# A hybrid attention, convolution and expert layer: chunk-by-chunk waits ahead of two matmul stages, and a shared last step

## The reference, cut to what matters

```python
h = rms_norm(x, norm1) * (1.0 + sc1) + sh1
q, k, v, u = project(h, w_in, q_norm, k_norm)
attn = context_attention(...) or latent_attention(...)   # 512 wide
conv = conformer_conv(u, ...)                            # 512 wide
x = x + g1 * (jnp.concatenate([attn, conv], axis=-1) @ w_out)
h2 = rms_norm(x, norm2) * (1.0 + sc2) + sh2
x = x + g2 * peer(h2, peer_wq, peer_keys, peer_u, peer_v)

def conformer_conv(u, w_dw, b_dw, ln_g, ln_b, w_pw):
    ...                                    # gated, then a depthwise convolution: y
    y = jax.nn.silu(layer_norm(y, ln_g, ln_b))
    return y @ w_pw
```

## Time and profile before

| what | us |
|---|---|
| median of 3 runs (lowest to highest) | 1766.24 (1764.96 to 1771.95) |
| the profiled execution's own time | 1766.6 |
| its span, first to last instruction | 1764.8 |
| PE busy in it | 1672.8 |
| DVE busy in it | 1558.7 |
| ACT busy in it | 861.6 |
| POOL busy in it | 644.9 |

### The profile page before, as it was taken

One profiled execution on the slowest core, in us unless ns is written; L12 is line 12 of the kernel. 1 busy time (PEld: TensorE's weight loads), 2 busy tenths in 40 slices (PEclk: granted clock), 3 DMA queues, 4 the chain that ended last, 5 costly groups with the idle time before them and its releaser, 6 DMA issues.

```text
span 1764.8 us, 29813 instructions
## 1 busy us (share of the span) xinstructions
PE 1672.8 (95%) x9344; PEld 1408.6 (80%) x9344; DVE 1558.7 (88%) x3209; ACT 861.6 (49%) x2416; POOL 644.9 (37%) x636
## 2 busy tenths in 40 slices
PE   6999998999957887999999999999999999999997
PEld 4566776966636776999999999999998998999986
DVE  3887863389999987999999999999999999999999
ACT  3221563337787876444444444444444444444443
POOL 0000000033548884444344444344444443443441
PEclk9999999999987998999999999999999999999999
DMA  8343102211114789999999999999999999999996
GB/s 352 119 146 118 73 1 75 72 49 60 48 42 161 195 265 314 405 408 400 399 409 398 395 413 400 399 410 399 402 411 393 393 402 400 397 404 408 398 385 213
DMA packets 128788, 508.79 MB, mean 288 GB/s; under 512 B 8528, under 2 KB 63568, under 8 KB 79312
## 3 DMA queue, kind: packets, MB, share of 16 engines
q0 software_dynamic: 36864, 268.45, 37.5%
q1 hardware_dynamic: 91568, 239.37, 36.5%
q10 hardware_dynamic: 288, 0.13, 0.0%
HBM read 480.00 MB, written 27.92 MB: 288 GB/s over the span
## 4 chain that ended last, share of the span: by engine, by line
DVE 33%; DMA 23%; PE 22%; issue 18%; POOL 2%; ACT 1%; DVEq 1%; POOLq 0%; SPq 0%; ACTq 0%
DMA slab<-table,ixr 21%; DVE slab L1604 9%; PE psum L461 7%; DVE ulo L1517 5%; PE psum L693 3%; DVE slab L1554 3%; DVE slab L1593 3%; PE psum L781 2%; DVE vlo L1580 2%; DVE slab L1588 2%; PE psum L462 2%; DVE wlo L1576 2%; PE psum L624 1%; POOL slab L1697 1%; DVE slab L1431 1%
## 5 line engine op out<-in xcount | busy, mean ns | idle before, releaser
L1697 POOL DMA_INDIRECT slab<-table,ixr x256 | 422.9, 1652 | 619.7 <-DVE slab L1604 547.3
L802 PE MATMUL psum<-hhi,uhi 128*128 128x384 f32 x1008 | 339.0, 336 | 1.1 <-issue 0.9
L802 PE MATMUL psum<-hhi,ulo 128*128 128x384 f32 x1008 | 338.2, 336 | 0.0
L802 PE MATMUL psum<-hlo,uhi 128*128 128x384 f32 x1008 | 337.6, 335 | 0.0
L1593 DVE SCALAR_TENSOR_TENSOR slab<-slab,h2tok 128x1024 f32<-128x1024 f32 x256 | 312.7, 1222 | 27.6 <-DMA slab<-table,ixr 27.6
L1604 DVE SCALAR_TENSOR_TENSOR slab<-slab,cf 128x1024 f32<-128x1024 f32 x252 | 323.7, 1284 | 14.5
L816 PE MATMUL psum<-vhi,whi 128*128 128x512 f32 x768 | 299.8, 390 | 11.2 <-DVE wlo L1576 11.2
L816 PE MATMUL psum<-vhi,wlo 128*128 128x512 f32 x768 | 302.3, 394 | 0.0
L816 PE MATMUL psum<-vlo,whi 128*128 128x512 f32 x768 | 302.0, 393 | 0.0
L461 PE MATMUL psum<-slab 128*128 128x512 f32 x464 | 240.6, 600 | 6.9 <-ACT slab L943 5.2
L1104 ACT CAST whi<-slab 128x384 fp32r<-128x384 f32 x128 | 65.8, 514 | 307.2 <-DVE slab L1588 307.2
(11 more groups left out here) (216 smaller groups left out, 2790.4 us busy)
## 6 DMA issues: line engine op xcount, KB each, us to landing
slab<-ublk SPq DMA_DIRECT2D x64, 1024.0 KB, 8.6
slab<-vtab SPq DMA_DIRECT2D x64, 1024.0 KB, 8.4
slab<-wblk SPq DMA_DIRECT2D x90, 512.0 KB, 4.5
slab<-g_dram SPq DMA_DIRECT2D x32, 768.0 KB, 9.2
g_dram<-slab SPq DMA_DIRECT2D x11, 2048.0 KB, 9.1
slab<-table,ixr POOLq DMA_INDIRECT x256, 9.2
x<-x_in SPq DMA_DIRECT2D x1, 2560.0 KB, 10.7
y_out<-x SPq DMA_DIRECT2D x5, 512.0 KB, 3.5
```

The source lines that it names most:

```text
L802: last = pe.matmul(psum[:, b, 0:ND], w[:, c, :], m[:, c, :], start=(m_ == 0), stop=(m_ == 3 * DC - 1))
L1697: pool.indirect_dma_start(out=rows[:, sl % GR, :], out_offset=None, in_=table, in_offset=bass.IndirectOffsetOnAxis(ap=ixr[:, half, sl % 8: ...
```

## The change

Three edits. (1) ScalarE's gate of chunk 0 stands ahead of the last two attention copies, the other three behind them, and the first pw block waits for each chunk of `y` at its use. (2) The first output block waits for seven chunks of `mlo` at its head and for the eighth at its use. (3) At the end, of each dense tile VectorE takes the low four chunks alone; the high four are scaled by ScalarE from PSUM to SBUF (`scaled_out`) and added to `x` by GpSimd. The transposes use more PSUM banks, in an order written out by hand; ScalarE's copies of the dense sums wait for `row_used` in place of `summed`; the last tile is stored in two halves.

```diff
@@ tensor
-            def linear(dst, w, src, chunks=DC, p0=T_L, fresh=None):
+            def linear(dst, w, src, chunks=DC, p0=T_L, fresh=None, gated=False):
                 for c in range(chunks):
                     if fresh is not None:
                         pe.wait_ge(h_ready, fresh + c + 1)
+                    if gated:
+                        pe.wait_ge(y_ready, c + 1)
                     last = both(dst, w[:, c, :], src[:, c, :], 0, p0, c == 0, c == chunks - 1)
...
-            pe.wait_ge(y_ready, CC)
             pe.wait_ge(tp_read, 4 * N_UNITS)
             for b in range(2):
                 pe.wait_ge(attn_ready, N_UNITS - 1 + b)
-                linear(lin[b % 2], weights(S_PW + b), y, CC, YP)
+                linear(lin[b % 2], weights(S_PW + b), y, CC, YP, gated=not b)
...
-            pe.wait_ge(mix_lo, DC)
-
             def out_block(j):
                 pe.wait_ge(out_lo, j + 1)
                 pe.wait_ge(lin_dve, max(j - 1, 0) + 1)
+                if not j:
+                    pe.wait_ge(mix_lo, DC - 1)
                 for c in range(DC):
+                    if not j and c == DC - 1:
+                        pe.wait_ge(mix_lo, DC)
...
-            for k in range(TILES):
-                if k < N_GATHER:
-                    pe.wait_ge(summed, k + 1)
-                else:
-                    pe.wait_ge(evacuated, k - N_GATHER + 1)
-                for half in range(2):
-                    if k:
-                        pe.wait_ge(fin_read, DC * (k - 1) + 4 * half + 4)
-                    for c in range(4):
-                        last = pe.transpose(psum[:, half, ...], final_src(k)[...], ident)
-                    last.then_inc(fin_tp, 1)
+            pe.wait_ge(summed, 1)
+            turn(0, 0)
+            turn(0, 1)
+            pe.wait_ge(evacuated, 1)
+            turn(2, 1)
+            pe.wait_ge(summed, 2)
+            turn(1, 0)
+            pe.wait_ge(evacuated, 2)
+            turn(1, 1)
+            pe.wait_ge(fin_read, 4)
+            turn(2, 0)
+            turn(3, 1)
+            pe.wait_ge(fin_read, 8)
+            turn(3, 0)
+            pe.wait_ge(evacuated, 3)
+            pe.wait_ge(fin_scaled, 4)
+            turn(4, 1)
+            pe.wait_ge(fin_read, 12)
+            turn(4, 0)
@@ scalar
                 lay(un)
-                if un:
+                if 0 < un < N_UNITS - 1:
                     mixed(un - 1)
-            mixed(N_UNITS - 1)
-            for c in range(CC):
+
+            def gate(c):
                 act.wait_ge(yscaled, c + 1)
                 act.activation(y[:, c, :], y[:, c, :], ACT.Silu, bias=V(V_LB + c), scale=V(V_LG + c)).then_inc(y_ready, 1)
+
+            gate(0)
+            mixed(N_UNITS - 2)
+            mixed(N_UNITS - 1)
+            for c in range(1, CC):
+                gate(c)
...
+            act.wait_ge(out_done, KEYS)
+            act.wait_ge(row_used, N_GATHER * SLOTS)
+            evacuate(2)
+            evacuate(3)
+            scale_out(0, 3)
+            evacuate(4)
+            scale_out(1, 7)
+            scale_out(2, 9)
@@ vector
-            for k in range(TILES):
-                ...
+            take(0, 0, 1)
+            take(0, 1, 2)
+            take(1, 0, 4)
+            take(1, 1, 5)
+            take(2, 0, 6)
+            take(3, 0, 8)
+            take(4, 0, 10)
@@ gpsimd
+            for n in range(N_DENSE):
+                for j in range(4):
+                    pool.wait_ge(fin_scaled, 4 * n + j + 1)
+                    xc, _ = final_x(N_GATHER + n, 4 + j)
+                    pool.tensor_tensor(xc, xc, scaled_out[:, 4 * n + j, :], ALU.add).then_inc(fin_added, 1)
@@ sync
+            for k in range(N_GATHER):
+                sp.wait_ge(fin_read, DC * (k + 1))
+                store(k, slice(0, DC))
+            for n in range(N_DENSE - 1):
+                sp.wait_ge(fin_read, DC * N_GATHER + 4 * (n + 1))
+                sp.wait_ge(fin_added, 4 * (n + 1))
+                store(N_GATHER + n, slice(0, DC))
+            sp.wait_ge(fin_added, 4 * N_DENSE)
+            store(TILES - 1, slice(4, DC))
+            sp.wait_ge(fin_read, DC * N_GATHER + 4 * N_DENSE)
+            store(TILES - 1, slice(0, 4))
+            sp.wait_ge(stored, 16 * (TILES + 1))
```

More of the change, by code:

```diff
@@ L268, in build @@
         wgt = view(36864, 4, ND)
+        scaled_out = view(33792, 4 * N_DENSE, P)
         slab_at = nc.lookup_mloc(slab).addr
@@ L301, in build @@
         ix_copied = sem("ix_copied"); dots = sem("dots"); gelued = sem("gelued"); coef = sem("coef");
-        summed = sem("summed"); evacuated = sem("evacuated"); fin_tp = sem("fin_tp"); fin_read = sem("fin_read"); stored = sem("stored")
+        summed = sem("summed"); evacuated = sem("evacuated"); fin_tp = sem("fin_tp"); fin_read = sem("fin_read"); fin_scaled = sem("fin_scaled"); fin_added = sem("fin_added"); stored = sem("stored")
         kv_stored = sem("kv_stored")
@@ L328, in hot_a_split, with final_bank, final_x @@
             return 1 if b % 4 == 3 else 2
+        def final_bank(k, half):
+            own = [2 + 2 * ORDER[N_GATHER + n] for n in range(N_DENSE)]
+            return {(0, 0): 0, (0, 1): 1, (2, 1): own[0], (1, 0): own[0] + 1, (1, 1): own[1], (2, 0): 0,
+                    (3, 1): own[1] + 1, (3, 0): 1, (4, 1): own[0], (4, 0): own[0] + 1}[k, half]
+        def final_x(k, c):
+            t = ORDER[k]
+            return x[:, c, t * P:(t + 1) * P], mod[:, M_G2 + c, int(t == TP):int(t == TP) + 1]
         def final_src(k):
@@ L424, in _, with store @@
             load_quad(quads - 1, 1, True)
-            for k in range(TILES):
+            def store(k, cols):
                 t = ORDER[k]
+                sp.dma_start(y_out[:, cols, t * P:(t + 1) * P], x[:, cols, t * P:(t + 1) * P]).then_inc(stored, 16)
+            for k in range(N_GATHER):
                 sp.wait_ge(fin_read, DC * (k + 1))
-                sp.dma_start(y_out[:, :, t * P:(t + 1) * P], x[:, :, t * P:(t + 1) * P]).then_inc(stored, 16)
-            sp.wait_ge(stored, 16 * TILES)
+                store(k, slice(0, DC))
[8 more added lines that the diff above has]
+            sp.wait_ge(stored, 16 * (TILES + 1))
         @block.tensor
@@ L829, in _, with turn @@
             outputs(KEYS - 1, JB - 1, False, True)
-            for k in range(TILES):
-                if k < N_GATHER:
-                    pe.wait_ge(summed, k + 1)
-                else:
-                    pe.wait_ge(evacuated, k - N_GATHER + 1)
-                for half in range(2):
-                    if k:
-                        pe.wait_ge(fin_read, DC * (k - 1) + 4 * half + 4)
-                    for c in range(4):
-                        last = pe.transpose(psum[:, half, c * P:(c + 1) * P], final_src(k)[:, (4 * half + c) * P:(4 * half + c + 1) * P], ident)
-                    last.then_inc(fin_tp, 1)
+            def turn(k, half):
+                for c in range(4):
+                    last = pe.transpose(psum[:, final_bank(k, half), c * P:(c + 1) * P], final_src(k)[:, (4 * half + c) * P:(4 * half + c + 1) * P], ident)
+                last.then_inc(fin_tp, 1)
+            pe.wait_ge(summed, 1)
[17 more added lines that the diff above has]
+            turn(4, 0)
         @block.scalar
@@ L1139, in _, with evacuate, scale_out @@
                 coefficients(n, jj, True)
[L1141 to L1144, removed]
+            def evacuate(k):
                 act.copy(final_src(k), bank(2 + 2 * ORDER[k], 2)).then_inc(evacuated, 1)
+            def scale_out(n, turned):
+                k = N_GATHER + n
+                act.wait_ge(fin_tp, turned)
+                for j in range(4):
+                    act.activation(scaled_out[:, 4 * n + j, :], psum[:, final_bank(k, 1), j * P:(j + 1) * P], ACT.Copy, scale=final_x(k, 4 + j)[1]).then_inc(fin_scaled, 1)
+            act.wait_ge(out_done, KEYS)
[6 more added lines that the diff above has]
+            scale_out(2, 9)
         @block.vector
@@ L1631, in _, with take @@
                 v.tensor_tensor(accs[k][:, 0, :], accs[k][:, 0, :], accs[k][:, 1, :], ALU.add).then_inc(summed, 1)
[L1632 to L1639, removed]
+            def take(k, half, turned):
+                v.wait_ge(fin_tp, turned)
+                for j in range(4):
+                    xc, scale = final_x(k, 4 * half + j)
+                    v.scalar_tensor_tensor(out=xc, in0=psum[:, final_bank(k, half), j * P:(j + 1) * P], scalar=scale, in1=xc, op0=ALU.mult, op1=ALU.add).then_inc(fin_read, 1)
+            take(0, 0, 1)
[5 more added lines that the diff above has]
+            take(4, 0, 10)
         @block.gpsimd
```

## The result

The changed kernel ran in 1760.79 us (median of 9), the kernel before beside it in 1770.27 us; the ratio is 0.9946 with a 95% interval of 0.9932 to 0.996, that is 9.6 us less, where 9.1 were forecast. A second series on another occasion gave 0.9947 (0.9928 to 0.9966). Single times of either kernel spread over 8 to 9 us (1764.96 to 1772.89 before, 1755.19 to 1764.53 after), so steps of 1 us must be read from traces, between two points of the same trace.

A forecast was written before the change was run, and what follows sets the result against it. No single engine bounds the span: the chain passes through VectorE, DMA and TensorE, and the stores' transfer nearly fills the end. 8.44 + 0.7 = 9.1 us, from 1766.24 to 1757.1 us; range 1753.8 to 1761.6.

The forecast's parts named there:

- Edit 1, the start: Ahead of the pw stage: TensorE's first pw matmul starts at 265.43 instead of 270.28, 4.85 us.
- The new waits within block 0: First pw block: each later gate is there when its chunk wants it, the first by 0.04 us; TensorE isn't stopped.
- The row's 1.28 us for the table load: ScalarE ahead of gate 0: load priced from the trace; at the skill page's 2.7 us the sum would be 7.7.
- Edit 1, the clock: First three pw chunks: with idleness of 0.3 us, not 5.1, no half clock is expected; 1.79 us less.
- Edit 2: Between pw stage and output projection: the 1.81 us wait for the eighth chunk closes wholly.
- The sum of both: Output projection starts at 282.74 instead of 291.18, 8.44 us, carried in full by the stages behind.
- Edit 3: At the end: VectorE frees 3.1 us, but the stores' nearly continuous transfer lets only 0.7 us through.
- The low clock: Rival, pw stage: half clock comes all the same and 1.79 us come back; 7.3 us, 1758.9; chance 0.12.
- VectorE's bound: Rival, end: stores overlap better and the end follows VectorE; 11.5 us in all, 1754.7; chance 0.08.
- the mutual exclusion: Rival, end: GpSimd and VectorE exclude each other, VectorE's 7.3 us become 12.7; 7.0 us in all, 1759.2; chance 0.05.
- part of the shift being given back: Rival, stages behind: another phase brings one more stretch of half clock, costing 1.7 us; 1758.8; chance 0.12.
- The sign of being wrong: Expert loop: its 1044 us changing by more than 2 would show the forecast wrong.

The follow-up runs named there:

- the added matmuls: Kernel before, with five more 512-column matmuls in TensorE's hole ahead of the pw stage; projection 27.1 us after the last turned copy, 28.8 before.
- edit 2 alone: Kernel before, with only the last `mlo` chunk waited for at its use; ratio 0.9997 (0.9987 to 1.0008).
- edit 3 alone: Kernel before, with only the end shared among VectorE, ScalarE and GpSimd; ratio 0.9999 (0.999 to 1.0009).
- edit 1 alone: Kernel before, with only the moved gate and the chunk-wise wait for `y`; ratio 0.9965 (0.9951 to 0.9979), 6.2 us.
- the changed kernel's second trace: The whole change run once more against the kernel before, on one chip with two other kernels; ratio 0.9947 (0.9928 to 0.9966).
- the last of the end's variants: Changed kernel, tiles 0 and 1 stored in halves, last two dense tiles together in 1 KB rows; ratio to the kernel before 0.9942 (0.9925 to 0.9958).
- edits 1 and 2, second time: Kernel before with the first two edits, without the shared end, run again; ratio 0.995 (0.9934 to 0.9967), the first time 0.9968.

## Why the prediction was right, step by step

*The size.* 9.1 us forecast, 9.6 measured (7.1 to 12.0 by the first interval, 6.0 to 12.7 by the second), 9.0 in the traces' own steps. That the times came within 0.5 us is luck, with intervals of 5 us; the agreement that counts is that of the steps. The absolute time was 3.7 us off: 1757.1 was forecast from the 1766.24 of three runs, and the median of nine was 1770.27 for the kernel before and 1760.79 for the changed one, 0.8 us inside the stated range.

*Edit 1, the start.* 4.85 us: shown, with 4.8 in the trace. From the start of the last turned copy to the first pw matmul 3.08 us (259.67 to 262.75), forecast 3.04. The new waits within block 0 stop nothing that can be seen: the second chunk starts 1.16 us after the first, as against 1.19 with the added matmuls, where no such wait stands, and the others 1.07 to 1.09 us apart. The row's 1.28 us for the table load held: from the end of the copy ahead of it to the start of the gate 1.31 us passed (260.15 to 261.46). The 2.7 us that the Trainium skill, "ScalarE: Activation LUTs", section "What ACT_TABLE_LOAD costs", gives for a switch of tables include a drain beside the load, as the page says; no such drain shows in this trace, so it is there that the two differ, and not in the load.

*Edit 1, the clock.* The mechanism is shown, by the added matmuls. The term of 1.79 us fits the execution that it was read from: fifteen chunks took 18.01 us there and 16.31 in the changed kernel, 1.7 us less. It looks too small as a mean: the same 5.2 us of idleness cost 2.8 us in the trace of edit 2 alone and 2.1 in that of edit 3 alone, and the shorter ones of 2.8 and 3.1 us cost 1.4 and 3.1. This is the one step that was mis-sized; one profile gave one draw of it.

*Edit 2.* 1.8 us: shown in the traces (from the first pw matmul to the projection 17.3 us with both edits, 19.2 with edit 1 alone). In the trace of edit 2 alone the clock took 1 us of it back; whether it did so in the timed runs isn't shown. *The sum of both*, 8.44 us, is 8.4 in each trace.

*Edit 3.* 0.7 us forecast, 0.6 and 0.7 in the traces. That it is the transfer, and not VectorE or GpSimd, is shown from three sides: VectorE's earlier end and GpSimd's work away change nothing beyond these 0.6 us, an earlier first store does. VectorE's 3.1 us were freed as said; ScalarE's scaling took 0.28 us for 0.26, GpSimd's add 0.43 for 0.45.

*The rivals.* The low clock came in none of the eight traces that have edit 1 whole. VectorE's bound and the mutual exclusion fell. For part of the shift being given back there is no sign, but the untouched stretch scatters by 8 us, so a loss of a microsecond there stays open. I priced a disturbance of that stretch at 1.7 us, from the clock alone; most of its scatter is the expert loop's (1061.6 to 1067.0 us), whose cause stays open. The sign of being wrong that I named for it, a change of the loop by more than 2 us, was ill chosen: with the same code the loop took 3.0 us longer in the changed kernel's second trace and 5.2 in the last of the end's variants, so it would have spoken without a cause in the change.

## What to carry to other kernels

Ask of every idle stretch of TensorE ahead of dense matmuls what it costs in clock as well as in waiting: here the clock was 1.4 to 3.1 us on top of 2.8 to 5.2 of waiting, and an edit that only shortens the idleness may get almost nothing. Where the last results are stored, count the transfer from the first store to the last against the engines' work; where the DMA share was near 1.0 there, an earlier first store and longer rows shortened the end, and faster engines gave only what gaps between the stores had left. Where times scatter by more than an edit is worth, measure it between two points of the same trace, and don't subtract spans.

## What the runs showed that I had not expected

In three of the eight traces with the old end, TensorE's clock fell within it, and the end took 17.4 to 17.8 us instead of 16.6. One of them (edits 1 and 2, second time), windows before and within, then VectorE's timeline:

```profile
1743.00:1745.00 2.00, 0.83 (x9) 0.63 (x8) 2.00 (x7) 1.13 (x2) 0.00 (x0) 1.00 0.00 0
1745.30:1754.00 8.70, 8.00 (x31) 5.18 (x29) 8.08 (x31) 1.41 (x2) 0.00 (x0) 0.50 0.64 182
...
1750.71 2.16 DVE L1647 SCALAR_TENSOR_TENSOR x<-psum,mod,x 128x128 f32<-128x128 f32 x8 [0.18 <-PE psum L843]
1753.11 2.16 DVE L1647 SCALAR_TENSOR_TENSOR x<-psum,mod,x 128x128 f32<-128x128 f32 x8 [0.24 <-PE psum L843]
```

At half clock the four transposes of a half take as long as VectorE's four instructions (1.03 and 1.08 us), and with two banks in turn VectorE begins to wait for them. TensorE was busy in the old end only in short groups, with holes of 0.3 to 1.2 us; that these holes bring the fall is a guess. In the six traces with the new end, whose transposes all lie within 5.2 us (1739.56 to 1744.78 in the changed kernel), the clock fell only behind them, and none took over 16.0 us. So edit 3 may be worth a microsecond more in some executions. Three of eight against none of six proves little, and no run here forces it.
